# Feed-forward of a two-block transformer: the inner values of chunks 1 to 9 turned by DMA transposes of 16-bit halves instead of by TensorE

## What is computed

```python
def swiglu(x, w_gate, w_up, w_down):
    return (jax.nn.silu(x @ w_gate) * (x @ w_up)) @ w_down

# first block, SEQ = 256, D_MODEL = 1024, D_FF = 2816
h = h + FFN_RES * swiglu(rms_norm(h, ffn1_norm), ffn1_w_gate, ffn1_w_up, ffn1_w_down)
h = h + hybrid_mixer(...)
h = h + FFN_RES * swiglu(rms_norm(h, ffn2_norm), ffn2_w_gate, ffn2_w_up, ffn2_w_down)
# second block, for each of two layers
x = x + y                                  # mixer
x = x + memory_cross_attention(...)
x = x + swiglu_2(rms_norm_2(x, g_ffn), w_gate, w_up, w_down)
```

## Time and profile before

| | us |
|---|---|
| median of 3 runs | 1242.99 (1242.81 to 1243.23) |
| the profiled execution | 1241.81 |
| its span | 1240.0 |
| TensorE busy | 1226.4 |
| VectorE busy | 750.5 |
| ScalarE busy | 646.3 |
| mean DMA rate | 177 GB/s |

### The profile page before, as it was taken

How to read it: one execution, slowest core, us unless ns; L and a number is a source line. 1 busy time by engine, 2 the same in 40 slices (tenths; PEclk the granted TensorE clock), 3 DMA queues, 4 the chain that set the end, 5 groups by cost and what they waited for, 6 DMA issues and landing times.

```text
span 1240.0 us, 17462 instructions
## 1 busy us (share of the span) xinstructions
PE 1226.4 (99%) x5862; PEld 1010.6 (81%) x5862; DVE 750.5 (61%) x1005; ACT 646.3 (52%) x939; POOL 68.8 (6%) x122
## 2 busy tenths in 40 slices
PE   8999999998999999999999999999999999999998
PEld 7888888886788888888888788888888887888887
DVE  5564555668875555457668766655546666655554
ACT  6454445557665444446666566543445456644432
POOL 0540000000000000000220110000000001000000
PEclk9999999999999999999999999999999999999999
DMA  7866564643455775654555425765564543665662
GB/s 223 251 217 198 178 198 147 205 157 103 136 170 159 241 225 183 202 186 148 175 170 170 154 67 183 213 195 184 191 196 149 181 153 102 204 201 183 192 196 92
DMA packets 166737, 219.43 MB, mean 177 GB/s; under 512 B 13680, under 2 KB 108640, under 8 KB 166560
## 3 DMA queue, kind: packets, MB, share of 16 engines
q1 hardware_dynamic: 164608, 213.70, 54.4%
q0 software_dynamic: 1648, 4.75, 1.3%
q10 hardware_dynamic: 432, 0.33, 0.1%
HBM read 217.68 MB, written 1.05 MB: 176 GB/s over the span
## 4 chain that ended last, share of the span: by engine, by line
PE 95%; DVE 3%; ACT 1%; issue 1%; DMA 0%; POOL 0%; SPq 0%; ACTq 0%; DVEq 0%; POOLq 0%
PE bank L1768 29%; PE bank L1770 29%; PE bank L1769 29%; PE bank L1824 2%; PE bank L1862 2%; DVE sb_wl L1164 1%; PE bank L2031 1%; PE bank L2047 1%; DVE sb_shared L1367 0%; PE bank L2018 0%; ACT sb_probs L1083 0%; DVE sb_scores L1350 0%; PE bank L2016 0%; DMA sb_raw<-w_up 0%; PE bank L1941 0%
## 5 line engine op out<-in xcount | busy, mean ns | idle before, releaser
L1164 DVE TENSOR_TENSOR sb_wl<-sb_raw,sb_wh 128x1024 fp32r<-128x1024 f32 x403 | 485.0, 1222 | 222.8 <-ACT sb_wh L654 217.6
L654 ACT ACTIVATE sb_wh<-sb_raw 128x1024 fp32r<-128x1024 f32 (+1 forms) x405 | 419.3, 1055 | 236.1 <-DMA sb_raw<-ffn_w_up 74.5
L1768 PE MATMUL bank<-sb_wh,sb_aTh 128*128 128x512 f32 (+1 forms) x1132 | 443.2, 392 | 1.2 <-DVE sb_wl L1164 0.7
L1770 PE MATMUL bank<-sb_wh,sb_aTl 128*128 128x512 f32 (+1 forms) x1132 | 435.1, 384 | 0.0
L1769 PE MATMUL bank<-sb_wl,sb_aTh 128*128 128x512 f32 (+1 forms) x1132 | 434.3, 384 | 0.0
L1770 PEld LDWEIGHTS bank<-sb_wh,sb_aTl 128*128 128x128 f32 x1132 | 212.8, 188 | 43.0
L1768 PEld LDWEIGHTS bank<-sb_wh,sb_aTh 128*128 128x128 f32 x1132 | 213.2, 188 | 41.8 <-issue 1.6
L1769 PEld LDWEIGHTS bank<-sb_wl,sb_aTh 128*128 128x128 f32 x1132 | 213.3, 188 | 39.4
L1768 PE MATMUL bank<-sb_wh,sb_hTh 128*128 128x512 f32 x320 | 124.9, 390 | 0.0
L1770 PE MATMUL bank<-sb_wh,sb_hTl 128*128 128x512 f32 x320 | 124.7, 390 | 0.0
L1769 PE MATMUL bank<-sb_wl,sb_hTh 128*128 128x512 f32 x320 | 124.5, 389 | 0.0
(11 more groups left out here) (235 smaller groups left out, 834.4 us busy)
## 6 DMA issues: line engine op xcount, KB each, us to landing
sb_raw<-ffn_w_down SPq DMA_DIRECT2D x88, 256.0 KB, 3.0
sb_raw<-w_gate SPq DMA_DIRECT2D x88, 256.0 KB, 3.4
sb_raw<-w_up SPq DMA_DIRECT2D x88, 256.0 KB, 4.1
sb_raw<-w_down SPq DMA_DIRECT2D x88, 256.0 KB, 2.9
sb_raw<-ffn_w_gate SPq DMA_DIRECT2D x87, 256.0 KB, 3.4
sb_raw<-ffn_w_up SPq DMA_DIRECT2D x87, 256.0 KB, 4.1
sb_raw<-w_in SPq DMA_DIRECT2D x80, 256.0 KB, 3.0
sb_raw<-e_w_in SPq DMA_DIRECT2D x40, 256.0 KB, 3.0
```

The lines of the kernel that those rows point to most:

```text
L654: return act.activation(dst, src, ACT.Copy, scale=scale)
L1164: dve.tensor_tensor(wl[:, u % NSPLIT, :], raw[:, u % NRAW, :], wh[:, u % NSPLIT, :].bitcast(F32), ALU.subtract).then_inc(low_done, 1)
L1768: pe.matmul(dst, lh, w_hi, start=start, stop=False)
L1770: return pe.matmul(dst, ll, w_hi, start=False, stop=stop)
```

## The change

Chunks 0 and 10 of each feed-forward keep the transposes on TensorE. For chunks 1 to 9:

- ScalarE copies the values of `hid`, seen as 16-bit halves, into two planes, all first halves and then all second halves (`planes`, in a part of `probs` that is free in the feed-forward).
- SyncE issues one DMA transpose of the 128 x 1024 16-bit values, eight blocks of 128 x 128, into `planesT`.
- VectorE joins the halves again with two copies into `hT` (in `probsT`), ScalarE rounds `hT` to `hTh`, VectorE subtracts to get `hTl`; both now read SBUF where they read bank 6.

```diff
+        hid_halves = scores[:, :, :].bitcast(U16).rearrange("p t (c h) -> p h t c", h=2)[:, :, :, 0:FC]
+        planes = probs[:, 2, :].bitcast(U16)
+        planesT = probs[:, 3, :].bitcast(U16)
+        hT = probsT[:, 0, :].rearrange("p (k t) -> p k t", k=2)
+        hT_halves = probsT[:, 0, :].bitcast(U16).rearrange("p (k t r h) -> p h k t r", k=2, t=NT, h=2)
...
                 for g in range(2):
+                    if g == 1 and between is not None:
+                        sem_, n = between
+                        sp.wait_ge(sem_, n)
                     sp.dma_start(dst[:, g], ffn_w[f][g][:, 2 * i:2 * i + 2, bass.ds(FC * chunk, FC)])\
...
-                with sp.Fori(0, NFC - 1, 1) as c:
+                def turn_hidden():
+                    sp.dma_start_transpose(planesT.rearrange("p (b r) -> p b r", r=P), planes).then_inc(planes_turned, 16)
+
+                def load_pass(c, turn=None):
                     for i in range(4):
-                        load_gate_up(u + 4 + i, f, i, c + 1, c)
+                        if i == 2 and turn is not None:
+                            load_gate_up(u + 4 + i, f, i, c + 1, c, (planes_done, (NFC - 2) * f + turn))
+                            turn_hidden()
+                        else:
+                            load_gate_up(u + 4 + i, f, i, c + 1, c)
                     for k in range(2):
                         load_down(u + 8 + k, f, 2 * c + k, c)
+
+                load_pass(0)
+                load_pass(1)
+                with sp.Fori(2, NFC - 1, 1) as c:
+                    load_pass(c, c - 1)
                 for k in range(2):
                     load_down(u + 64 + k, f, 2 * (NFC - 1) + k)
+                sp.wait_ge(planes_done, (NFC - 2) * (f + 1))
+                turn_hidden()
...
+                def planes_step(c):
+                    act.wait_ge(h_ready, 2 * NFC * f + 2 + 2 * c)
+                    act.wait_ge(planes_turned, 16 * ((NFC - 2) * f - 1) + 16 * c)
+                    for h in range(2):
+                        ins = copy(planes.rearrange("p (h t c) -> p h t c", h=2, t=NT)[:, h], hid_halves[:, h])
+                    ins.then_inc(planes_done, 1)
+
+                def turned_step(c):
+                    act.wait_ge(hT_joined, (NFC - 2) * f + c)
+                    copy(hTh[:, :, :], hT).then_inc(ht_high, 1)
...
                     silu_step(c + 1)
+                    if not tail_chunk:
+                        planes_step(c + 1)
...
+                def join_step(c):
+                    dve.wait_ge(planes_turned, 16 * (NFC - 2) * f + 16 * c)
+                    turned = planesT.rearrange("p (h t k r) -> p h k t r", h=2, t=NT, k=2)
+                    for h in range(2):
+                        ins = dve.tensor_copy(hT_halves[:, h], turned[:, h])
+                    ins.then_inc(hT_joined, 1)
...
                 with pe.Fori(1, NFC - 2, 1) as c:
+                    pe.wait_ge(h_ready, 2 * NFC * f + 2 + 2 * c)
                     gate_up(c)
...
-                    transpose_hidden(c + 1)
```

More of the change, by code:

```diff
@@ L25 @@
 I32 = mybir.dt.int32
+U16 = mybir.dt.uint16
 ACT = mybir.ActivationFunctionType
@@ L276, in two_block_kernel @@
         ht_low = sem("ht_low")
+        planes_done = sem("planes_done")
+        planes_turned = sem("planes_turned")
+        hT_joined = sem("hT_joined")
         acc_done = sem("acc_done")
@@ L429, in load_quarters, with load_gate_up @@
                         sp.dma_start(dst, w[:, k0:k0 + 2, 256 * h:256 * h + 256]).then_inc(loaded[(u + i) % NRAW], 16)
-            def load_gate_up(u, f, i, chunk, c=0):
+            def load_gate_up(u, f, i, chunk, c=0, between=None):
                 free_raw(u, c)
@@ L717, in silu_step, with ht_step, body @@
                            .then_inc(silu_done, 1)
-                def ht_step(c, dst):
-                    act.wait_ge(ht_psum, NFC * f + c + 1)
+                def ht_step(n, dst):
+                    act.wait_ge(ht_psum, 2 * f + n)
                     copy(dst, bank[6][:, :]).then_inc(ht_high, 1)
-                def body(c, dst):
+                def planes_step(c):
[7 more added lines that the diff above has]
+                    copy(hTh[:, :, :], hT).then_inc(ht_high, 1)
+                def body(c, turned, tail_chunk=False):
                     for i in range(4):
                         split(u + 4 + i, c)
+                    if turned:
+                        turned_step(c)
                     act.wait_ge(units_used, u + 8 + 6 * c)
                     silu_step(c + 1)
+                    if not tail_chunk:
+                        planes_step(c + 1)
                     for i in range(2):
                         split(u + 8 + i, c)
-                    ht_step(c + 1, dst)
                 if f > 0:
@@ L748, in ffn @@
                 splits(u + 2, 2)
[L749 to L753, removed]
+                ht_step(1, hTh[:, :, :])
+                body(0, False)
+                with act.Fori(1, NFC - 2, 1) as c:
+                    body(c, True)
+                body(NFC - 2, True, True)
+                ht_step(2, aTh[:, 6:8, :])
                 if tail is not None:
@@ L1233, in ht_step, with turned_step, body @@
                     dve.tensor_tensor(low, bank[6][:, :], high.bitcast(F32), ALU.subtract).then_inc(ht_low, 1)
-                def body(c, low, high):
-                    for i in range(4):
-                        split(u + 4 + i, c)
+                def join_step(c):
[4 more added lines that the diff above has]
+                    ins.then_inc(hT_joined, 1)
+                def turned_step(c):
+                    dve.wait_ge(ht_high, NFC * f + c + 1)
+                    dve.tensor_tensor(hTl[:, :, :], hT, hTh[:, :, :].bitcast(F32), ALU.subtract).then_inc(ht_low, 1)
+                def body(c, turned):
+                    for i in range(3):
+                        split(u + 4 + i, c)
+                    if turned:
+                        join_step(c)
+                    split(u + 7, c)
+                    if turned:
+                        turned_step(c)
                     mul_step(c + 1)
@@ L1240, in body @@
                         split(u + 8 + i, c)
-                    ht_step(c + 1, low, high)
                 splits(u, 2)
@@ L1246, in ffn @@
                 ht_step(0, hTl[:, :, :], hTh[:, :, :])
-                with dve.Fori(0, NFC - 2, 1) as c:
-                    body(c, hTl[:, :, :], hTh[:, :, :])
-                body(NFC - 2, aTl[:, 6:8, :], aTh[:, 6:8, :])
+                body(0, False)
+                with dve.Fori(1, NFC - 2, 1) as c:
+                    body(c, True)
+                body(NFC - 2, True)
+                ht_step(NFC - 1, aTl[:, 6:8, :], aTh[:, 6:8, :])
                 if tail is not None:
@@ L1893, in ffn @@
                 down_unit(0, 1)
-                transpose_hidden(1)
                 with pe.Fori(1, NFC - 2, 1) as c:
+                    pe.wait_ge(h_ready, 2 * NFC * f + 2 + 2 * c)
                     gate_up(c)
```

## The result

The changed kernel took 1312.57 us (median of 4 runs, 1310.53 to 1313.91), the kernel before beside it 1242.9 us. The ratio is 1.0559, with an interval of 1.0543 to 1.0574: 70 us slower. The profiled execution took 1311.74 us, its span was 1310.0 us, and the granted clock averaged 0.984.

What follows compares the result with a forecast made beforehand. TensorE bound the kernel before; after the change a circle without it would: 14.26 + 6.0 = 20.26 us a pass against 16.80, 36 x 3.46 = 125 us lost, 1243.0 + 125 = 1368 us. Range 1260 to 1530 us.

Steps and rivals of the forecast that it cites:

- A circle through the other engines: Feed-forward loop: steps from one transpose's landing to the next, without TensorE, set the pass: 14.26 us plus L.
- The sum of 14.26 us: Feed-forward pass: VectorE, ScalarE and SyncE steps from a transpose's landing to the next one's issue, 14.26 us.
- A3': Third gate/up weight unit of the next pass; its load, two issues taking 0.93 us, precedes the transpose on SyncE.
- D2': Second down weight unit of the next pass; its load was put at 3.43 us in the circle.
- D2: Second down weight unit of a pass; its splits were put at 1.10 us on ScalarE and 1.23 on VectorE.
- L: Time from the DMA transpose's issue on SyncE to its landing; taken as 6.0 us, usual upper end 10.
- a plain landing of 4.1: SyncE's queue: landing of a 256 KB load directly behind another, 4.1 us, taken as the transpose's price if plain.
- rival 2: Feed-forward passes: the transpose runs like a plain load, L 3.0 to 4.1, time 1260 to 1311 us; chance 0.25.
- the floor that the clock sets: TensorE behind a hole: half clock for about 3.3 us costs 1.6 us; pass floor about 18.7 us, costed at nothing.
- The ceiling: TensorE: most the change can give, 36 sets of transposes removed at 0.44 us each, 15.8 us.
- the signs that I named: Profile after: TensorE idle before 36 down products, pass minus L near 14.3 us, lower DMA share, clock near 0.5 behind holes.
- the estimate was 1299 us: Whole kernel if a DMA transpose is as fast as a regular DMA: L 4.1 us, circle 18.4 us, 1299 us.

Runs made afterwards that it cites:

- experiment 1: Changed kernel with the DMA transpose issued a pass earlier, behind the load of D2' instead of behind A3'; 1273.07 us, ratio 1.025.
- experiment 4: Changed kernel with ScalarE's plane copies moved behind its splits of the next pass's last two gate/up units; 1278.38 us, ratio 1.0287.
- experiment 10: Changed kernel with each DMA transpose issued twice, the first into an unread buffer, ScalarE and VectorE waiting for both; 1347.41 us, ratio 1.0829.
- experiment 3: Changed kernel plus 32 spare sets of four TensorE transposes whose results are not read; 1319.94 us, ratio 1.0611.
- experiment 2: Changed kernel with the DMA transpose replaced by a plain DMA copy of the same 256 KB, values not turned; 1296.56 us, ratio 1.043.
- experiment 6: Experiment 1's kernel with join behind the first split of a pass, hTl and hTh behind the second; 1238.44 us, ratio 0.9967 to the kernel before.
- experiment 7: Experiment 6's kernel with the edit of experiment 4 added; 1231.84 us, ratio 0.9926 to the kernel before.
- experiment 8: Changed kernel with seven unread matmuls of zeros on TensorE ahead of its wait for hTl; 1314.06 us, ratio 1.0585.

## Why the prediction was right, and where it was off

1. **The sign and the mechanism held.** A circle through the other engines sets the middle passes, not TensorE: 21 of the 24 end with TensorE waiting for `hTl`. The chain shows each link in the order that the prediction gave, experiments 1 and 4 each cut it at another link, experiment 10 stretched it with a slope of 0.93, and in experiment 3 it hid four fifths of the work added to TensorE in those passes. Pass by pass in the changed kernel, the length of a middle pass less the time from the transpose's issue to the join is 14.0 to 14.3 us in 19 of the 24; the five others are those of point 5.

2. **The sum of 14.26 us was right**: 14.14 us in the pass shown. Link by link, from the chain and the timeline: landing to the end of the products 3.31 us (predicted 3.80, since the join pair took 0.80 instead of 1.0 and the instructions overlap), to the split 1.17 (1.10), the two splits of A3' 2.32 (2.33), 0.18 to SyncE (0.17), the load of D2' 3.60 (3.43), the two splits of D2 2.43 (2.33), to the transpose 1.13 (1.10).

3. **The term that was mis-sized is L.** I took 6.0 us, it was 4.2 in the median and 3.83 in the pass shown. I had added 2 us for small pieces, priced by ScalarE's queue in the earlier trace rows, on top of a plain landing of 4.1. The pieces are there: the page counts 51,696 packets under 512 bytes, 38,016 more than before, 1,056 for each transpose. But experiment 2 shows that all of the turning costs 0.7 us of landing. The plain landing too was lower than my bound, 3.5 against 4.1: the row of `ffn_w_up`, behind its gate load, was a poor neighbour; the plain copy lies between that row and the 3.0 of `ffn_w_down` in the earlier trace rows. 36 passes by 6.0 - 4.2 are 65 us, and the forecast missed by 55: the likeliest value, 1368 us, did not come, and it was the width of the range that took the result in.

4. **The first passes were priced like middle ones, and cost 24.4 us.** With L = 4.2 the sum would have been 14.26 + 4.2 = 18.46 a pass and 1243 + 36 x 1.66 = 1303 us; what was measured lies 10 us higher, just above rival 2's range of 1260 to 1311. At that price four passes lose 6.6 us: the first passes lost 17.8 more than that, the last ones 8.0 less, and the 28 between lost 45.9 where it gives 46.5. So two errors, at the two ends of the loop, partly cancel. I had placed the first transpose on the clock of a middle pass of before, at 110.49, with ScalarE starting silu at 0.20 us behind the down product. But at a feed-forward's head the loads lag. Already in the kernel before, silu of the third feed-forward's first pass starts at 780.42, its down product at 778.17, 2.25 us earlier (ScalarE's timeline, before):

```profile
779.45 1.06 ACT L654 ACTIVATE sb_wh<-sb_raw 128x1024 fp32r<-128x1024 f32 x1 [1.74 <-DMA sb_raw<-w_up]
780.42 0.83 ACT L716 ACTIVATE sb_junk<-bank,sb_rstd 128x256 f32<-128x256 f32 x2
```

It cost nothing there. After the change the same pass (down product at 814.75) has silu at 816.84, the planes behind it, and only then the split of A3'. ScalarE's, SyncE's and TensorE's rows:

```profile
816.84 0.82 ACT L744 ACTIVATE sb_junk<-bank,sb_rstd 128x256 f32<-128x256 f32 x2
819.01 1.15 ACT L682 ACTIVATE sb_probs<-sb_scores 128x512 uint16<-128x512 uint16 x2 [1.35 <-DVE sb_scores L1273]
820.07 2.94 ACT L682 ACTIVATE sb_wh<-sb_raw 128x1024 fp32r<-128x1024 f32 x3
```
```profile
829.55 1.26 SPq L469 DMA_TRANSPOSE sb_probs<-sb_probs  x1
```
```profile
835.86 0.79 PE L1833 MATMUL bank<-sb_wh,sb_hTh 128*128 128x512 f32 x1 [4.64 <-DVE sb_hTl L1292]
```

The split of A3' starts 5.3 us behind the down product, where the earlier trace rows have 0.9, and the transpose is issued 14.8 us behind it, where I had 11.1. In all four first passes, the length less the time from issue to join is 17.4 to 17.9 us, against 14.0 to 14.3 in most of the middle ones. In feed-forwards 1 and 2 the landing is late as well: the join comes 5.47 and 8.48 us after the issue, beside GpSimd's loads, and the longest hole, 9.85 us, is there. Moving the transpose alone left the first passes at 20.5 to 25.4 us (experiment 1); with join and `hTl` taken forward too they are 16.3 to 17.0 us (experiments 6 and 7).

5. **The clock was costed at nothing, and costs some passes.** Around a hole of 2.52 us that ends at 873.90 (TensorE's timeline, then the windows):

```profile
873.90 0.49 PE L1833 MATMUL bank<-sb_wh,sb_hTh 128*128 128x512 f32 x1 [2.52 <-DVE sb_hTl L1292]
```
```profile
872.00:875.00 3.00, 1.10 (x4) 0.93 (x5) 2.55 (x5) 1.69 (x4) 0.00 (x0) 0.91 0.22 62
875.00:878.00 3.00, 3.00 (x9) 2.32 (x8) 1.20 (x2) 2.71 (x4) 0.00 (x0) 0.52 0.35 126
878.00:881.00 3.00, 3.00 (x15) 2.46 (x14) 2.38 (x3) 1.07 (x1) 0.00 (x0) 1.00 0.51 167
```

From 875 to 878 the granted clock is 0.52, the level of 1.2 GHz, and TensorE does 9 matmuls where it does 15 in the next 3 us. TensorE is then late with the rest of that pass, which ends without a hole, and at the head of the next one silu waits for TensorE, not the reverse (ScalarE's timeline):

```profile
892.16 0.84 ACT L744 ACTIVATE sb_junk<-bank,sb_rstd 128x256 f32<-128x256 f32 x2 [1.52 <-PE bank L1835]
```

The pass that begins there took 18.90 us. This happens at the head of five of the 24 middle passes, all in feed-forwards 3 and 4, each behind a pass in which TensorE ran 3 to 5 us at half the clock. In these five the length less the time to the join is 14.7 to 15.1 us, about 4 us over the others together. But a hole does not always bring it. Of the 21 holes that end a middle pass, 1.1 to 2.6 us long, three (2.52, 2.41 and 1.78 us) are followed by about 3 us at half the clock and the others by none, the longest of them included (TensorE's timeline, then the window behind it):

```profile
1278.78 0.49 PE L1833 MATMUL bank<-sb_wh,sb_hTh 128*128 128x512 f32 x1 [2.56 <-DVE sb_hTl L1292]
```
```profile
1280.00:1283.00 3.00, 3.00 (x15) 2.44 (x13) 1.32 (x2) 3.00 (x5) 0.00 (x0) 1.00 0.34 112
```

I had put the floor that the clock sets at 18.7 us a pass and called it nothing, which was right for a circle of 20.3 and wrong for one of 18.1. In experiment 8 no middle pass has a slow stretch, and they are 0.3 us shorter in the mean; 5.8 of the 7.2 us come from feed-forwards 3 and 4, where the slow stretches had been. Why the clock falls behind one hole and not behind another stays open.

6. **Small ones.** The transpose holds SyncE's queue 1.24 us against 0.42 for a load; I had counted only its landing. In the changed kernel's chain the hold is no link of its own, but in experiment 1 it was part of the second path. The last pass of each feed-forward had no hole and gained 0.35 us; its transpose stands behind the last down loads, with no load of a next chunk in front of it. The ceiling was 36 x 0.48 = 17.3 us rather than 15.8, as passes fell from 16.80 to 16.32 in experiment 7. Of the signs that I named, two came out otherwise: the granted clock near 0.5 does not stand behind each hole, and the share of the DMA engines did not fall (SyncE's queue took 54.4% before and 56.7% after, 53.8% with the plain copy of experiment 2).

7. **The rule of the Trainium skill** (Advanced Engine Details and Errata, X-Bar Transpose), that a transposing DMA is as fast as a regular one on this chip, comes close and does not hold exactly here. The measured pair is 4.2 against 3.5 us to landing, and 1.24 against 0.49 us on the issuing queue. By that rule the estimate was 1299 us, 14 under what was measured and nearer than mine.

So the idea pays a little (7 in 1,000, experiment 7); it loses 70 us through where its steps stand in the queues of three engines.

## What to carry to other kernels

When a step is moved off the busiest engine, follow the new steps around until they reach themselves, counting each instruction that merely stands in front on an in-order engine: a circle that leaves the busiest engine out sets the pass, however much slack each engine has on the whole. Price the first pass of a loop from its own rows, not from a middle one. And when the circle is cut in one place, look for the next longest path before forecasting the gain: here two single cuts gave about half each and left the first passes as they were; the earlier transpose with its consumers moved forward gave back all of the loss, and the second cut on top of it 7 us more.

## What was not expected of the hardware

- A DMA transpose of 256 KB of 16-bit values within SBUF landed 4.2 us (median) after its issue and held its queue 1.24 us; a plain copy of the same bytes took 3.5 and 0.49. It was carried as some 1,056 packets under 512 bytes (the plain copy has 16).
- Two of them issued directly behind each other cost only 1.13 us more than one.
- While GpSimd's loads were under way or just issued, the same transpose landed after 8 to 12 us, and one held SyncE for 3.15 us. Moving those loads moved the late landing with them. Plain copies (experiment 2) had a landing of 8.2 us too, and weight loads one of 9.5 us (experiment 7) and, in the kernel before, 10.7 us, so it isn't the turning. What in the DMA engines holds it back was not measured.
- Of 21 holes of 1.1 to 2.6 us in TensorE's work, one to a pass, three (1.78, 2.41 and 2.52 us) were followed by some 3 us at a granted clock of about 0.5, and the one of 2.56 us was not.
